# A diagonal state space recurrence taken by blocks of four tokens inside a two-block transformer kernel on Trainium2

## The reference, cut to what matters

```
lam_bar = exp(lam * dt)                       # one complex number per state
b_bar   = ((lam_bar - 1) / lam) * B
bu[s]   = b_bar @ u[s]
x[s]    = lam_bar * x[s-1] + bu[s]            # over all 256 tokens
y[s]    = real(C @ x[s]) + d_skip * u[s]
y       = gelu(y);  y = y * sigmoid(y @ glu_w + glu_b)
```

## Time and profile before

| What | us |
|---|---|
| median of 3 runs | 1814.4 (1813.58 to 1816.68) |
| the profiled execution, its own time | 1816.94 |
| its span | 1815.1 |
| TensorE busy | 1381.8 |
| VectorE busy | 590.1 |
| ScalarE busy | 396.0 |
| GpSimd busy | 257.6 |
| from the end of unit 0 to the start of unit 7 | 34.1 to 186.4 |

### The profile page before, as it was taken

How to read it: one execution, slowest core, us unless ns; L and a number is a source line. 1 busy time by engine, 2 the same in 40 slices (tenths; PEclk the granted TensorE clock), 3 DMA queues, 4 the chain that set the end, 5 groups by cost and what they waited for, 6 DMA issues and landing times.

```text
span 1815.1 us, 26805 instructions
## 1 busy us (share of the span) xinstructions
PE 1381.8 (76%) x11672; PEld 917.5 (51%) x11672; DVE 590.1 (33%) x842; ACT 396.0 (22%) x494; POOL 257.6 (14%) x285
## 2 busy tenths in 40 slices
PE   6887987799979998866666665698988566656655
PEld 4333776679869796422232322397964232322322
DVE  4998135533654944000000000439451000000001
ACT  3111532333444341101010100244421000101011
POOL 5556372000000610000000000005100000000000
PEclk9998998899999998989888889799989988888896
DMA  9311112435445249999999999933399999999996
GB/s 351 129 47 47 47 64 98 146 140 178 151 143 178 93 152 395 424 427 425 426 427 425 427 425 428 359 127 106 117 381 409 427 425 428 425 428 425 427 424 275
DMA packets 85999, 516.29 MB, mean 284 GB/s; under 512 B 6192, under 2 KB 6320, under 8 KB 52912
## 3 DMA queue, kind: packets, MB, share of 16 engines
q1 hardware_dynamic: 82560, 509.22, 69.1%
q0 software_dynamic: 864, 3.41, 0.5%
q10 hardware_dynamic: 2512, 2.75, 0.5%
HBM read 514.31 MB, written 1.05 MB: 284 GB/s over the span
## 4 chain that ended last, share of the span: by engine, by line
DMA 43%; PE 33%; DVE 7%; ACT 3%; issue 2%; POOL 1%; SPq 1%; DVEq 0%; ACTq 0%; POOLq 0%
DMA ring<-in_w_down 20%; DMA ring<-in_w_gate 18%; PE dense L1341 7%; PE dense L1343 7%; PE dense L1342 7%; DMA ring<-in_w_up 4%; PE bank L1745 2%; PE bank L1770 2%; PE dense L1358 2%; DVE work L1174 1%; PE dense L1375 1%; SPq L532 1%; DVE work L1165 1%; DVE ring_parts L1079 1%; PE dense L1701 1%
## 5 line engine op out<-in xcount | busy, mean ns | idle before, releaser
L1745 PE MATMUL bank<-ring,work 128*32 128x256 f32 x2688 | 202.4, 455 | 144.8 <-DMA ring<-in_w_up 87.6
L1745 PEld LDWEIGHTS bank<-ring,work 128*32 128x32 f32 x2688 | 92.0, 126 | 250.2 <-DMA ring<-in_w_up 108.3
L1271 DVE TENSOR_TENSOR work<-work,bank 128x256 f32<-128x256 f32 x32 | 13.5, 421 | 564.3 <-ACT work L865 564.3
L865 ACT ACTIVATE work<-bank 128x256 f32<-128x256 f32 x32 | 12.3, 384 | 750.7 <-PE bank L1745 750.7
L727 ACT ACTIVATE ring_parts<-ring 128x4096 fp32r<-128x4096 f32 (+1 forms) x40 | 137.6, 3447 | 143.1 <-DMA ring<-in_w_in 47.1
L1079 DVE TENSOR_TENSOR ring_parts<-ring,ring_parts 128x4096 fp32r<-128x4096 f32 (+1 forms) x33 | 137.5, 4178 | 90.1 <-ACT ring_parts L727 90.1
L1745 PE MATMUL bank<-work 128*32 128x256 f32 x1408 | 104.9, 451 | 73.5 <-DMA work<-in_w_up 46.0
L643 POOL TENSOR_TENSOR work<-work 128x128 f32<-128x128 f32 x64 | 24.2, 399 | 939.9 <-PE bank L1753 782.2
L1770 PE MATMUL bank<-ring,work 128*32 128x256 f32 x1344 | 90.6, 415 | 59.5 <-DMA ring<-in_w_down 55.1
L1341 PE MATMUL dense<-xT_parts,ring_parts 128*128 128x256 f32 x448 | 130.1, 290 | 2.7 <-DVE ring_parts L1079 2.7
L1342 PE MATMUL dense<-work_parts,ring_parts 128*128 128x256 f32 x448 | 129.0, 288 | 0.0
(11 more groups left out here) (300 smaller groups left out, 2319.3 us busy)
## 6 DMA issues: line engine op xcount, KB each, us to landing
ring<-in_w_gate SPq DMA_DIRECT2D x42, 2048.0 KB, 41.0
ring<-in_w_up SPq DMA_DIRECT2D x42, 2048.0 KB, 41.0
ring<-in_w_down SPq DMA_DIRECT2D x42, 2048.0 KB, 40.7
work<-in_w_gate SPq DMA_DIRECT2D x22, 2048.0 KB, 40.6
work<-in_w_up SPq DMA_DIRECT2D x22, 2048.0 KB, 40.7
work<-in_w_down SPq DMA_DIRECT2D x22, 2048.0 KB, 41.0
ring<-in_w_in SPq DMA_DIRECT2D x18, 2048.0 KB, 7.9
ring<-in_even_w_in SPq DMA_DIRECT2D x10, 2048.0 KB, 19.8
```

Source lines behind the costliest of these rows:

```text
L1745: last = mm(WB[0][32 * q:32 * q + 32, 256 * (j % 2):256 * (j % 2) + 256], xeT[:, 4 * (j // 2) + k, :], w[:, k * D + 256 * q:k * D + 256 * ...
```

## The change

The recurrence is taken over 64 blocks of four tokens (`SL = 4`, `SB = 64`). With w = lam_bar, the state at the end of a block is w^4 times the one before plus a sum over the block's four tokens with B times w^3, w^2, w and w (powers kept in `bpow`), and the output of a block is C times powers of w (`cpow`) on the state before the block, plus a 128 x 128 matrix (`within`) on the block's own 128 numbers (32 channels x 4 tokens), in which the skip term is the diagonal. VectorE builds `bpow` and `cpow` (four powers each). TensorE turns B by eight transposes in unit 0 (`b_transposes`), puts `u` into blocks with 64 matmuls against an identity of 32 x 32 (`blocks`, step U), transposes `bpow` (G, 8 steps of 4), builds `within` from 11 small matmuls per tile (T, 4 steps of 4 tiles), computes the drives (V, 4 steps of 8 matmuls of 64 columns), the outputs (Y, 4 steps of 12 matmuls of 64 columns) and puts the result back by token (`by_token`, step R, 64 matmuls). `SSM_STEPS` says ahead of which quarter each stands: key 4(m-1)+c is quarter c of unit m. VectorE then scans four times over 4 tiles x 64 blocks where it scanned 16 times over 256 tokens; a zero factor at each tile's first block keeps the tiles apart. GpSimd computes phases of 64 block starts for 4 tiles at once, four times. ScalarE copies every intermediate result out of PSUM. The buffers move: `cpow` lies where k and v go, so ScalarE empties units 3 and later only behind the last output's gelu. The load of `row` moves on GpSimd's queue behind `ssm_done`.

```diff
-STATE_SLOT = [0, 1] + [4 + (23 - 4) * n // (SSM_TILES - 1) for n in range(SSM_TILES)]
+SSM_STEPS = {1: "U", 2: "G0 G1 G2 G3", 3: "G4 G5 G6 G7", 4: "V0 V1", 5: "T0 T1", 6: "T2 T3", 9: "Y0 V2", 10: "V3", 11: "Y1",
+             13: "Y2", 14: "Y3", 16: "R"}
...
+            lo, hi = VEC["ssm_d"]
+            for i in range(SL):
+                gp.dma_start(skip[32 * i:32 * i + 32, :].rearrange("p (j c) -> p j c", j=4),
+                             a["vectors"][:, lo:hi].rearrange("(j m) c -> m j c", j=4)).then_inc(skip_in, 16)
...
+            for c in range(4):
+                angle = cs[:, :, 4 * SB * c:4 * SB * (c + 1)]
+                own.link(g.tensor_tensor(angle[:, 1, :].rearrange("p (t b) -> p t b", t=4),
+                                         cn("block_start").unsqueeze(1).to_broadcast([P, 4, SB]),
+                                         small[:, 0, 4 * c:4 * c + 4].unsqueeze(2).to_broadcast([P, 4, SB]), ALU.mult))
+                own.link(g.tensor_tensor(angle[:, 0, :], angle[:, 1, :], cn("quarter").to_broadcast([P, 4 * SB]), ALU.add))
+                own.link(g.tensor_tensor(whole, angle, cn("round").unsqueeze(1).to_broadcast([P, 2, 4 * SB]), ALU.add))
+                own.link(g.tensor_tensor(whole, whole, cn("unround").unsqueeze(1).to_broadcast([P, 2, 4 * SB]), ALU.add))
+                g.tensor_tensor(angle, angle, whole, ALU.subtract).then_inc(frac_ready, 1)
+                gp.wait_ge(frac_ready, c + 1)
...
+            gp.dma_start(row[:], a["post_norm"][0:1, :].partition_broadcast(P)).then_inc(row_in, 16)
...
+            for k in range(2):
+                act.wait_ge(bmat_ps, 1)
+                s.activation(bmat[:, 8 * k:8 * k + 8].rearrange("p t f m -> p (t f m)"), WB[k][:], ACT.Copy).then_inc(bmat_sb, 1)
...
+            act.wait_ge(unit_done, 1)
+            s.activation(u_steps, DP[0][:].rearrange("p z (c b i) -> p (z c) i b", c=2, i=SL), ACT.Copy).then_inc(dense_out, 1)
             act.wait_ge(masks_set, 1)
+            for j in range(4):
+                blocks_in(j)
+            for k in range(SSM_TILES // 2):
+                bpow_transposed(k)
             for c in range(4):
+                sincos(c)
+            tok_out(1, q_tok, 0, HD ** -0.5)
+            tok_out(2, q_tok, 512, HD ** -0.5)
+            for c in range(4):
+                gelu(c)
+            tok_out(3, k_tok, 0)
+            for i in range(SL):
+                tokens_out(i)
+            tok_out(4, k_tok, 512)
+            high_part(9)
+            tok_out(5, v_tok, 0)
+            high_part(10)
+            tok_out(6, v_tok, 512)
...
+            def times(z, re, im):
+                own.go(tt(by_re, z, over(re), ALU.mult))
+                own.link(tt(by_im, z, over(im), ALU.mult))
+            dve.wait_ge(bmat_sb, 2)
+            z = bmat.rearrange("p t f m -> p f t m")
+            for i in reversed(range(SL)):
+                times(z, sm(3), sm(4))
+                z = pair(B_AT + 32 * i)
+                own.go(tt(z[:, 0], by_re[:, 0], by_im[:, 1], ALU.subtract))
+                own.link(tt(z[:, 1], by_re[:, 1], by_im[:, 0], ALU.add))
+            v.memset(stat[:, 7, 0:1], 0.0).then_inc(bpow_ready, 1)
...
+            dve.wait_ge(cmat_in, 16)
+            times(cmat, sm(11), sm(13))
+            z = pair(C_AT)
+            own.go(tt(z[:, 0], by_re[:, 0], by_im[:, 1], ALU.subtract))
+            own.link(stt(z[:, 1], by_im[:, 0], -1.0, by_re[:, 1], ALU.mult, ALU.subtract))
+            for d in range(1, SL):
+                times(z, sm(3), sm(4))
+                z = pair(C_AT + 32 * d)
+                own.go(tt(z[:, 0], by_re[:, 0], by_im[:, 1], ALU.add))
+                own.link(tt(z[:, 1], by_re[:, 1], by_im[:, 0], ALU.subtract))
+            v.memset(stat[:, 7, 0:1], 0.0).then_inc(cpow_ready, 1)
+            tt(steps, sm(2).unsqueeze(2).to_broadcast([P, SSM_TILES, SB]),
+               cn("not_first").unsqueeze(1).to_broadcast([P, SSM_TILES, SB]), ALU.mult).then_inc(dve_own, 1)
+            own.n += 1
+            dve.wait_ge(skip_in, 16 * SL)
+            for t in range(SSM_TILES):
+                dve.wait_ge(within_ps, t // 4 + 1)
+                stt(within[t], ident, skip[:, 4 * (t % 4) + t // 4:4 * (t % 4) + t // 4 + 1], WB[2 + t // 4 % 2][:, P * (t % 4):P * (t % 4) + P], ALU.mult,
+                    ALU.add).then_inc(within_sb, 1)
+            own.settle()
...
+            for c in range(4):
+                here = slice(4 * SB * c, 4 * SB * (c + 1))
+                cosb = cs[:, 0:1, here].to_broadcast([P, 2, 4 * SB])
+                sinb = cs[:, 1:2, here].to_broadcast([P, 2, 4 * SB])
+                drive = WB[c % 2][:].rearrange("p (f n) -> p f n", f=2)
+                st = state[c % 2]
+                dve.wait_ge(cs_ready, c + 1)
+                dve.wait_ge(drive_ps, c + 1)
+                if c >= 2:
+                    dve.wait_ge(y_ps, c - 1)
+                own.go(tt(st, drive, cosb, ALU.mult))
+                tt(by_sin, drive, sinb, ALU.mult).then_inc(drive_used, 1)
                 own.settle()
+                dve.wait_ge(drive_used, c + 1)
+                own.go(tt(by_cos[:, 0, :], st[:, 0, :], by_sin[:, 1, :], ALU.add))
+                own.link(tt(by_cos[:, 1, :], st[:, 1, :], by_sin[:, 0, :], ALU.subtract))
+                r = steps[:, 4 * c:4 * c + 4, :].rearrange("p t b -> p (t b)")
                 for f in range(2):
+                    own.go(v.tensor_tensor_scan(st[:, f, :], r, by_cos[:, f, :], 0.0, ALU.mult, ALU.add))
                 own.settle()
+                own.go(tt(by_cos, st, cosb, ALU.mult))
+                own.link(tt(by_sin, st, sinb, ALU.mult))
+                tt(st[:, 0, :], by_cos[:, 0, :], by_sin[:, 1, :], ALU.subtract).then_inc(state_ready, 1)
+                tt(st[:, 1, :], by_cos[:, 1, :], by_sin[:, 0, :], ALU.add).then_inc(state_ready, 1)
+                dve.wait_ge(state_ready, 2 * c + 2)
...
+            tiles_of = lambda c: range(4 * c, 4 * c + 4)
+            def b_transposes(_):
+                pe.wait_ge(bmat_in, 16)
+                for c in range(4):
+                    for f in range(2):
+                        last = tr(WB[c // 2][:].rearrange("p (c j f m) -> p c f j m", c=2, j=4, f=2)[:, c % 2, f], b_rows[:, c, f, :],
+                                  ident)
+                last.then_inc(bmat_ps, 1)
+            def blocks(_):
+                pe.wait_ge(dense_out, 1)
+                pe.wait_ge(bmat_sb, 2)
+                for c in range(4):
+                    for i in range(SL):
+                        for j in range(4):
+                            r = slice(32 * j, 32 * j + 32)
+                            last = mm(WB[j][32 * i:32 * i + 32, SB * c:SB * c + SB], ident[r, r],
+                                      u_steps[r, c, i, :], start=True, stop=True)
+                last.then_inc(u_ps, 1)
+            def bpow_transposes(k):
+                if k == 0:
+                    pe.wait_ge(bpow_ready, 1)
+                    pe.wait_ge(u_sb, 4)
+                if k >= 2:
+                    pe.wait_ge(bt_sb, k - 1)
+                    for t in range(2):
+                        last = tr(WB[2 + k % 2][:, (2 * f + t) * P:(2 * f + t + 1) * P], bpow[f][:, 2 * k + t, :], ident)
+                last.then_inc(bt_ps, 1)
+            def within_blocks(c):
+                if c == 0:
+                    pe.wait_ge(cpow_ready, 1)
+                if c >= 2:
+                    pe.wait_ge(within_sb, 4 * (c - 1))
+                else:
+                    pe.wait_ge(bt_sb, SSM_TILES // 2 - 1 + c)
+                for t in tiles_of(c):
+                    o = WB[2 + c % 2][:, P * (t % 4):P * (t % 4) + P]
+                    for i in range(1, SL):
+                        mm(o[32 * i:32 * i + 32, 0:32 * i], bmat[:, t, 0, :], cn("none")[:, 0:32 * i], start=True, stop=True)
+                    for f in range(2):
+                        for i in range(SL):
+                            last = mm(o[32 * i:32 * i + 32, 32 * i:P], bmat[:, t, f, :], cpow[f][:, t, 0:P - 32 * i],
+                                      start=f == 0, stop=f == 1, skip_group_check=True)
+                last.then_inc(within_ps, 1)
+            def drives(c):
+                if c == 0:
+                    pe.wait_ge(bt_sb, SSM_TILES // 2)
+                if c >= 2:
+                    pe.wait_ge(drive_used, c - 1)
+                for f in range(2):
+                    for t in tiles_of(c):
+                        last = mm(WB[c % 2][:, (4 * f + t % 4) * SB:(4 * f + t % 4 + 1) * SB], bpow[f][:, t, :],
+                                  u_blocks[:, t, :], start=True, stop=True)
+                last.then_inc(drive_ps, 1)
+            def outputs(c):
+                pe.wait_ge(state_ready, 2 * c + 2)
+                if c < 2:
+                    pe.wait_ge(within_sb, 4 * (3 + c))
+                else:
+                    pe.wait_ge(yb_sb, c - 1)
+                    pe.wait_ge(within_sb, SSM_TILES)
+                for t in tiles_of(c):
```

(61 more changed lines are left out.)

172 lines of the change are left out of this document (52 added, 120 removed).

## The result

| | before | after |
|---|---|---|
| median, us | 1814.8 (4 runs, 1813.6 to 1816.7) | 1788.1 (4 runs, 1786.5 to 1790.5) |
| span of the profiled execution, us | 1815.1 | 1788.7 |
| start of unit 7, us | 186.4 | 158.3 |

The ratio is 0.9854, interval [0.9838, 0.9869]: 26.7 us faster. I had forecast 9.4 us and a range down to 1794, so the sign was right and the size was wrong by almost three. The four executions of the kernel after lie 4 us apart, and the profiled one is the slowest of them, so the 28.1 us at unit 7 against 26.4 us at the end is within what executions differ by.

What follows compares the result with a forecast made beforehand. Bound: TensorE's work plus waits for VectorE and low clock, 152.3 us. New sum: 1.8 + (82.8 + 1.8) quarters + 24.8 small + 7.0 G + 16.0 V and Y + 5.3 wait + 3.4 clock = 142.9, so 1805.0 us; range 1794 to 1821.

Steps and rivals of the forecast that it cites:

- Price of the small tiles: U, T and R on TensorE: 608 records at 0.041 us each, 24.8 us together, ends 16.4 and 32.8.
- Transposes: Eight in unit 0 and 32 in G on TensorE, four per 0.88 us: 1.8 + 7.0 us.
- Clock: TensorE's low clock in the stage: one stretch after the G0 wait and one more, 3.4 us.
- The rival that sparse arrays would not hold the clock: In the stage, waits go but the clock stays low: 1812 us, no measurable change; chance 16%.
- The wait at G0: TensorE at the first G step waits for VectorE's powers of B: 5.3 us, bounds 0 and 9.
- V and Y: Drives and outputs on TensorE: 80 matmuls of 64 columns at 0.20 us, 16.0 us.
- the quarters: 24 dense quarters on TensorE with 12 breaks instead of 18: 82.8 + 1.8 us.
- no wait at T0 or Y0: First T and Y steps cost no wait: 3 us of cover at T0, three quarters (10.4 us) before Y0.
- the move of `row`: Load on GpSimd's queue moves behind `ssm_done`; only the first norm reads it; priced at nothing.
- The slower rival: Small tiles of U, T and R run one after another, 48.5 us: 1823.4 us; chance 17%.
- the signs that the prediction named: Unit 7 near 177 us, U and R records 0.04 apart, T step 3.6, GpSimd phases done near 45, VectorE busy 75.
- the account of the stage before: Old stage of 152.3 us: quarters with breaks 85.5, `bu` and `cy` 32.5, waits 23.1, low clock 11.2.

Runs made afterwards that it cites:

- the late phases: Changed kernel with GpSimd's phases held back until C's powers are ready and unit 1 emptied before the sines: 1779.7 us, ratio 0.9814 to the kernel before.
- the worst order: Changed kernel with R's 64 small matmuls done five times, the four matmuls of one 32 x 32 tile following each other: 1804.8 us, one run.
- four extra bursts: Changed kernel with four extra copies of step R, one ahead of each of four later quarters: 1796.6 us, one run.

## Why the prediction was wrong

The forecast for the time from 34.1 us to unit 7 was 142.9; measured from the same point it is 124.2. The mechanism was right, waits and the clock behind them; the sum went wrong in the terms that were to be added on TensorE.

- **Price of the small tiles: the step that failed most.** I took the middle between 0.027 and 0.054 us per record, 24.8 us for U, T and R; they took 11.0. Both ends were wrong for U and R: the lower one let only four tiles run side by side, while U and R visit sixteen tiles of 32 x 32, and a record cost 0.011. For T the right unit was not the record but the column tile with most columns: 0.44 us per 32 channels, 7.0 us in all, measured 8.2 with one stop for instructions. The rows for both were there: 0.11 us per 128 columns and four column tiles side by side. The Trainium skill (TensorE: Matmul & The Clock Gate, Measured speedup vs the span model) has about 4 ns per further tile; the 0.011 us per record, a matmul and its weight load, is nearer to that than to the 25 ns per matmul of the section that I had cited. That floor does not hold here: 128 records went by in 1.40 us.
- **Transposes: a row misread.** I counted two records per transpose and priced four at 0.88 us; it is eight. The sentence in the description of the kernel that a float32 matmul stands as two records does not hold for them. G and the eight in unit 0 were priced 8.8 us and would take 4.4 at full clock. That is 4.4 us of error.
- **Clock.** I left 3.4 us of it; one stretch came back, 1.7 us. The rival that sparse arrays would not hold the clock fell: it is 1.00 through U, T, V, Y and R.
- **The wait at G0.** Right in kind and place, 5.3 us forecast, 6.6 measured. B's powers were ready at 49.0 and not 53.6, but TensorE was there at 42.5 and not 48.3, so that the size came out near is luck: two errors of 4.6 and 5.8 us cancelled. The parts of the sum were right. VectorE began at 24.8 (forecast 26), its powers alone take 14.9 (14.6), and GpSimd had 13.5 us left (13), by its times with the late phases, where it runs alone. What was off is adding them up: 14.9 us of work on VectorE took 24.2, so 9.3 us were lost and not 13.5. Both engines slow each other down, yet some 4 us of GpSimd's work went by at no cost. What makes that possible stays open.
- **V and Y** 17.5 us for 16.0; the quarters 83.7 for 84.6; no wait at T0 or Y0, as said. Unit 0 ended at 33.9 for 35.9, by the transposes at half their price and by weights that landed 1.0 us earlier, for which the move of `row` was priced at nothing: I looked only at who reads it and at GpSimd's queue, not at what its 512 KB share at the start.
- **The slower rival** needed the tiles to run one after another; even in the worst order they took 0.032 us per record, half of what it needed.

Of the signs that the prediction named, the one wait at G0, none at T0 or Y0 and GpSimd's end near 45 us came. The others did not: records of U and R stand 0.011 us apart and not 0.04, a T step takes 1.8 us and not 3.6, VectorE is busy 59.6 us and not 75, and unit 7 begins at 158 and not 177.

What I did get was the account of the stage before: quarters, branch and waits came from rows, the clock was what they left (11.2 us, of which the slowed rows show 9.0), and the gain came from the two terms that it named, the waits and the clock. Had I put 11.0 and 4.4 into the sum, TensorE would have been at G0 4.7 us earlier and waited that much longer: 142.9 - 13.8 - 4.4 + 4.7 = 129.4, or 1791.5 us. At unit 7 there are then 5.2 us left between 129.4 and 124.2: a wait of 6.6 where the corrected sum has 10.0, 1.7 less of low clock, 1.0 from the weights and 0.9 from the quarters, less 1.5 more for V and Y and 0.5 for G's short waits; 0.2 are rounding. At the end it is 3.4.

## What to carry to other kernels

Price packed small matmuls by the stream of the fullest tile first, not by the record. That gave T. For U and R it is only a lower bound: eight records per tile at 0.10 us are 0.8 us, an estimate from the earlier trace rows, and they took 1.4. Check how many records one instruction of each kind leaves before dividing. Where VectorE and GpSimd both feed a chain that TensorE waits for, put the one that is not needed yet behind the other: here one wait instruction and a swap gave 7 to 8 us more. A stall ahead of TensorE can cost its length and then the low clock behind it, here 6.6 and 1.7 us, so collisions are dear. Where a change moves the start as well, compare stages from their own first instruction: unit 0 alone differed by 3 us between profiles.

## What the runs showed of the hardware that was not expected

A stream of small matmuls outruns the loading of instructions. Some 220 to 250 records (each a matmul and a weight load) go by at 0.011 us; then TensorE gets 16 KB, 256 instructions, per 3.5 to 4 us, or per 6.2 us while the DMA engines are full. A dense quarter of 3.5 us between bursts of 128 records is enough to refill, nearly: one stop of 0.7 us came in four extra bursts. And 32 x 32 tiles visited in turn run at three times the rate of the same matmuls grouped by tile, 0.011 and 0.032 us per record. T's tiles, which take all 128 rows and 32 columns, ran the same in either order.
